# Second block of a two-block transformer: norm scales applied behind the products, norm rows multiplied beside the root

## The reference, cut to what matters

```python
def rmsnorm(x, g):
    return x * rsqrt(mean(x * x) + 1e-6) * g

for l in range(DEPTH):
    h = rmsnorm(x, g_pre_mix[l])
    y = mixers(h @ w_in[l])                      # three attention-like mixers
    x = x + rmsnorm(y @ w_out[l], g_post_mix[l])
    h = rmsnorm(x, g_pre_ffn[l])
    gate, up = split(h @ w_ffn_in[l])            # 2 x 2816 columns
    f = (silu(gate) * up) @ w_ffn_out[l]
    x = x + rmsnorm(f, g_post_ffn[l])
    e = p[l] @ w_ple_up[l]                       # 256 -> 1024
    g = sigmoid(rmsnorm(x, g_ple_gate[l]) @ w_ple_gate[l])
    x = x + rmsnorm(e * g, g_ple_post[l])
```

## Time and profile before

| | |
|---|---|
| median of three runs | 1909.09 us (1905.82 to 1911.23) |
| profiled execution | 1908.69 us, span 1906.9 us |
| PE busy | 1708.8 us, 90% of the span |
| DVE busy | 1093.6 us, 57% |
| ACT busy | 720.8 us, 38% |
| chain that ended last | PE 78%, DVE 13%, ACT 5%, issue 3% |
| second block | from about 1085 us to the end |

### The profile page before, as it was taken

One profiled execution on the slowest core, in us unless ns is written; L12 is line 12 of the kernel. 1 busy time (PEld: TensorE's weight loads), 2 busy tenths in 40 slices (PEclk: granted clock), 3 DMA queues, 4 the chain that ended last, 5 costly groups with the idle time before them and its releaser, 6 DMA issues.

```text
span 1906.9 us, 19158 instructions
## 1 busy us (share of the span) xinstructions
PE 1708.8 (90%) x7483; PEld 1287.3 (68%) x7483; DVE 1093.6 (57%) x1659; ACT 720.8 (38%) x1084; POOL 0.2 (0%) x4
## 2 busy tenths in 40 slices
PE   2999889999997998899999869889997798899995
PEld 2545647788884446477888757768885677788874
DVE  7574558686655625585455456754554457554544
ACT  1122333334321123343344235743444556543444
POOL 0000000000000000000000000000000000000000
PEclk9998689999998996899999979889998899899997
DMA  8655324876854441247555633134563352335540
GB/s 320 244 192 196 110 84 153 304 272 241 281 204 143 177 155 66 70 163 258 170 169 197 228 74 126 45 133 163 170 241 132 118 149 74 133 118 170 176 166 22
DMA packets 216378, 314.98 MB, mean 165 GB/s; under 512 B 20308, under 2 KB 145628, under 8 KB 216160
## 3 DMA queue, kind: packets, MB, share of 16 engines
q1 hardware_dynamic: 216288, 313.76, 47.8%
HBM read 312.70 MB, written 1.05 MB: 165 GB/s over the span
## 4 chain that ended last, share of the span: by engine, by line
PE 78%; DVE 13%; ACT 5%; issue 3%; SPq 0%; DVEq 0%; DMA 0%; ACTq 0%
PE psum L537 18%; PE psum L538 18%; PE psum L539 17%; PE psum L503 10%; DVE tmp L1150 3%; PE psum L544 2%; DVE arena L1150 1%; ACT arena L2071 1%; PE psum L580 1%; PE psum L1033 1%; PE psum L523 1%; PE psum L524 1%; PE psum L525 1%; DVE arena L1147 1%; ACT arena L2074 1%
## 5 line engine op out<-in xcount | busy, mean ns | idle before, releaser
L539 PE MATMUL psum<-arena_parts,hT_parts 128*128 128x512 f32 x928 | 370.1, 399 | 0.0
L1147 DVE TENSOR_TENSOR gring_parts<-gring,arena_parts 128x2048 fp32r<-128x2048 f32 x116 | 260.4, 2288 | 86.0 <-ACT arena_parts L2074 86.0
L503 PE MATMUL psum<-gring,hT 128*128 128x512 f32 (+1 forms) x576 | 256.7, 605 | 12.4 <-DVE arena L1147 6.1
L538 PE MATMUL psum<-gring_parts,arena_parts 128*128 128x512 f32 x544 | 221.7, 408 | 0.0
L1147 DVE TENSOR_TENSOR arena_parts<-psum,ex_parts 128x256 fp32r<-128x256 f32 x108 | 45.2, 418 | 299.6 <-ACT ex_parts L2074 299.6
L2074 ACT ACTIVATE arena_parts<-gring 128x2048 fp32r<-128x2048 f32 x116 | 215.4, 1917 | 0.1
L537 PE MATMUL psum<-arena_parts,o_cat_parts 128*128 128x512 f32 x512 | 205.9, 402 | 7.2 <-DVE hT_parts L1147 7.2
L503 PEld LDWEIGHTS psum<-gring,hT 128*128 128x128 f32 x576 | 114.1, 202 | 140.1 <-issue 122.0
L539 PEld LDWEIGHTS psum<-arena_parts,hT_parts 128*128 128x128 f32 x928 | 177.5, 191 | 41.9
L538 PE MATMUL psum<-gring_parts,o_cat_parts 128*128 128x512 f32 x512 | 204.9, 400 | 0.0
L2074 ACT ACTIVATE ex_parts<-psum 128x256 fp32r<-128x256 f32 x108 | 41.3, 382 | 416.3 <-PE psum L580 416.3
(11 more groups left out here) (218 smaller groups left out, 2296.7 us busy)
## 6 DMA issues: line engine op xcount, KB each, us to landing
gring<-in_w_ada SPq DMA_DIRECT2D x24, 2048.0 KB, 9.9
gring<-in_w_ffn_in SPq DMA_DIRECT2D x44, 1024.0 KB, 8.8
gring<-in_w_gate SPq DMA_DIRECT2D x32, 1024.0 KB, 7.4
gring<-in_w_up SPq DMA_DIRECT2D x32, 1024.0 KB, 9.8
dring<-in_w_down SPq DMA_DIRECT2D x32, 1024.0 KB, 5.0
gring<-in_w_in SPq DMA_DIRECT2D x14, 2048.0 KB, 10.5
dring<-in_w_ffn_out SPq DMA_DIRECT2D x22, 1024.0 KB, 4.9
gring<-in_w_out SPq DMA_DIRECT2D x8, 2048.0 KB, 8.5
```

The source lines that it names most:

```text
L503: last = nc.tensor.matmul(ps[:, 0:n], hT[:, k, t * P:(t + 1) * P], w[:, k, 0:n], start=k == 0, stop=k == KT - 1)
L538: nc.tensor.matmul(ps, hi, w_rest, start=False, stop=False)
L539: return nc.tensor.matmul(ps, lo, w, start=False, stop=stop)
L1147: return nc.vector.tensor_tensor(o, a, b, op)
```

## The change

- Pre-norm before the feed-forward part and before the embedding gate: x itself is transposed and multiplied by the gain column. The square sum of x, its root and its reciprocal are made behind that (`scale_squares`, `scale_of`, `scale_root`, `scale_done`), and the reciprocal is applied to the products: as the scale of the Silu and of the Sigmoid activation, and as a column factor in `hid`.
- Post-norm: each half is first multiplied by the row alone, the second half between the variance and the reciprocal, that is beside the root; then one instruction multiplies by the reciprocal and adds to x (`gained_and_added`, `rms_var`, `rms_added`).
- The transposes of tile 1 (xT2) go between the two halves of gu(0, 0); the transposes xT3 go behind the embedding products of their tile.
- pg0 takes the place of pg1 in steps 9 and 10; pg1 is rounded in step 10 (ScalarE) and its rest made around hT3 (VectorE). pg0 lies where pg1 did, pg1 in the other weight buffer.
- The embedding products are read from PSUM by VectorE instead of being copied by ScalarE; pg takes banks 4 to 7.
- avcv of the following layer is rounded before the Sigmoids; its rest is made before them too.
- Table loads are asked for early by one-element activations (`table_of`).
- SP: the small parameters of the following layer wait for the last product pg(1, 1); before, for the last gu.

```diff
-IN_DOWN = ("avcv", "aq", "ak", "buv", "cqk", "wo0", "pg0")
+IN_DOWN = ("avcv", "aq", "ak", "buv", "cqk", "wo0")
...
             if name == "pg1":
-                return stage, T, ("gu1", NF - 2)
-            if name == "pg0":
-                return stage, T, ("e", 1, 1)
+                return stage, T, ("gu1", NF - 1)
             if name == "avcv":
-                return (FIRST[-1], T, ("dn1", NE - 2 + q)) if stage == SECOND[0] else (SECOND[0], T, ("pg", 1, 0))
+                return (FIRST[-1], T, ("dn1", NE - 2 + q)) if stage == SECOND[0] else (SECOND[0], T, ("e", 1, 1))
...
-                        transposed("xT2", o_cat, 0, 6, ("xn", "ffn", 0))
+                        transposed("xT2", x, 0, 6, ("x", "mix", 0))
...
             first_half_gu(stage, 0, range(4, 8))
+            transposed("xT2", x, 1, 2, ("x", "mix", 1))
             first_half_gu(stage, 0, range(4)).then_inc(tensor_done, T.step(("gu0", 0)))
-            transposed("xT2", o_cat, 1, 2, ("xn", "ffn", 1))
...
-                    ps = take(("e", t, h), A, 2 * t + h)
+                    ps = take(("e", t, h), V, 2 * t + h)
...
-            transposed("xT3", o_cat, 0, 4, ("xn", "ple", 0))
+                transposed("xT3", x, t, 4 + 2 * t, ("x", "ffn", t))
...
-                        tt(hid[:, t, :], up, sact[:, t, :], ALU.mult)...
+                        stt(hid[:, t, :], up, scale[:, t:t + 1], sact[:, t, :], ALU.mult, ALU.mult)...
...
+        def rms_added(name, t, y):
+
+            dve.wait_ge(scalar_done, A.at(V, (("post", name), "sqrt", t)))
+            nc.vector.reciprocal(rstd[:, TT + t:TT + t + 1], rstd[:, t:t + 1])...
+            dve.wait_ge(vector_done, V.now())
+            stt(x[:, t, :], y, rstd[:, TT + t:TT + t + 1], x[:, t, :], ALU.mult, ALU.add)...
+
+        def gained_and_added(name, row, t, y, banks):
+
+            for h in range(2):
+                ps, read = banks(h)
+                if h:
+                    rms_var(("post", name), t)
+                else:
+                    dve.wait_ge(scalar_done, A.at(V, (("post", name), "ss0", t)))
+                tt(y[:, t, h * N:(h + 1) * N], ps, rows[:, row, h * N:(h + 1) * N], ALU.mult)...
+            rms_added(name, t, y[:, t, :])
...
+            for t in range(TT):
+                gained_and_added("mix", 0, t, y2m, lambda h: (bank(V, ("wo", t, h)), ("read", ("wo", t, h))))
+                modulated("xT2", "hT2", t, g_ffn)
+                features_rest("hT2", t, h_hi[1])
+                scale_of("ffn", t)
+                scale_done("ffn", t)
...
+            for t in range(TT):
                 modulated("xT3", "hT3", t, g_ple)
                 features_rest("hT3", t, h_hi3)
+                scale_of("ple", t)
+                chunk_rest(stage, "pg1", t)
+            for t in range(TT):
+                scale_done("ple", t)
+            following = SECOND[l + 1] if l + 1 < DEPTH else None
+            if following:
+                for q in range(2):
+                    chunk_rest(following, "avcv", q)
...
+            act.wait_ge(vector_done, V.at(A, ("scale", "ffn", TT - 1)))
+            act_experts(NF, 1, first_gate, scaled, second_gate)
...
+            for t in range(TT):
+                scale_root("ple", t)
+            following = SECOND[l + 1] if l + 1 < DEPTH else None
+            if following:
+                for q in range(2):
+                    rounded_half(following, "avcv", q)
+            table_of(ACT.Sigmoid)
...
             gated(0, 0)
+            squares(0, 0)
             gated(0, 1)
+            table_of(ACT.Sqrt)
+            squares(0, 1)
+            root_of(("post", "ple"), rstd[:, 0:1], 0)
...
-                sp.wait_ge(tensor_done, T.of(SECOND[l - 1], ("gu1", NF - 1)))
+                sp.wait_ge(tensor_done, T.of(SECOND[l - 1], ("pg", 1, 1)))
```

More of the change, by code:

```diff
@@ L451, in program @@
         rsum2, rinv2, ngm2 = sc(TT * 2 * DH), sc(TT * 2 * DH), sc(TT * WH)
+        scale_ss, scale_var, scale, idle = sc(TT), sc(TT), sc(TT), sc(1)
         lprod = sc(2 * DQK)
@@ L1714, in pre_norm, with scale_of, scale_done @@
             dve.wait_ge(vector_done, V.now())
-        def post_norm(name, row, t, y, banks):
-            rms(("post", name), t, True)
+        def scale_of(name, t):
+            dve.wait_ge(scalar_done, A.at(V, (("scale", name), "ss", t)))
+            ts(scale_var[:, t:t + 1], scale_ss[:, t:t + 1], 1.0 / D, RMS_EPS, ALU.mult, ALU.add).then_inc(vector_done, V.step((("scale", name), "var", t)))
+        def scale_done(name, t):
+            dve.wait_ge(scalar_done, A.at(V, (("scale", name), "sqrt", t)))
+            nc.vector.reciprocal(scale[:, t:t + 1], scale_var[:, t:t + 1]).then_inc(vector_done, V.step(("scale", name, t)))
+            dve.wait_ge(vector_done, V.now())
@@ L1982, in embedded @@
+                tt(y2[:, t, n], y2[:, t, n], bank(V, ("e", t, h)), ALU.mult).then_inc(vector_done, V.step(("eg", t, h)))
+                V.also(("read", ("e", t, h)))
                 dve.wait_ge(vector_done, V.now())
-                tt(x[:, t, :], x[:, t, :], y2[:, t, :], ALU.add).then_inc(vector_done, V.step(("x", "ple", t)))
-                dve.wait_ge(vector_done, V.now())
-            following = SECOND[l + 1] if l + 1 < DEPTH else None
+                tt(gb[:, n], y2[:, t, n], rows[:, 0, n], ALU.mult).then_inc(vector_done, V.step())
@@ L2440, in act_second @@
             for t in range(TT):
-                for h in range(2):
-                    act.wait_ge(tensor_done, T.at(A, ("e", t, h)))
-                    ps = bank(A, ("e", t, h))
-                    copy((e2 if t == 0 else e2b)[:, h * N:(h + 1) * N], ps).then_inc(scalar_done, A.step(("read", ("e", t, h))))
-            for q in range(2):
-                rounded_half(stage, "pg0", q)
-            for t in range(TT):
-                act.wait_ge(vector_done, V.at(A, ("x", "ffn", t)))
-                sum_squares(("pre", "ple"), t, x)
-                modulated_T("xT3", "hT3", t, g_ple, hi=h_hi3)
+                act.wait_ge(vector_done, V.at(A, ("x", "ffn", t)))
@@ L2452, in gated @@
+                scale_squares("ple", t)
+                modulated_T("xT3", "hT3", t, g_ple, hi=h_hi3)
+            for t in range(TT):
+                scale_root("ple", t)
[4 more added lines that the diff above has]
+            table_of(ACT.Sigmoid)
             def gated(t, h):
                 act.wait_ge(tensor_done, T.at(A, ("pg", t, h)))
-                activate(y2[:, t, h * N:(h + 1) * N], bank(A, ("pg", t, h)), ACT.Sigmoid).then_inc(scalar_done, A.step(("sig", t, h)))
+                if h == 0:
+                    act.wait_ge(vector_done, V.at(A, ("scale", "ple", t)))
+                    act.sem_inc(waited)
+                activate(y2[:, t, h * N:(h + 1) * N], bank(A, ("pg", t, h)), ACT.Sigmoid, **scaled(t)).then_inc(scalar_done, A.step(("sig", t, h)))
```

111 lines of the change are left out of this document (56 added, 55 removed).

## The result

The changed kernel took 1862.74 us (median of four runs, 1858.2 to 1866.43); the kernel before, on the same chip, 1908.82 us (1905.82 to 1911.23). The ratio is 0.9758, 95% interval 0.9733 to 0.9784: 46 us less, where 40.5 were forecast. The profiled execution took 1862.91 us, its span 1861.1. TensorE's busy time fell from 1708.8 to 1697.8 us for the same number of instructions, so most of what went is idle time, the rest slow clock.

A forecast was written before the change was run, and what follows sets the result against it. TensorE was taken to be bound by waits at each layer's two joints and the second layer's entry, plus slow clock behind idle times. Gains 3.4 + 1.7 + 18.7 + 16.7 = 40.5 us gave 1868.5 us, range 1859 to 1879.

The forecast's parts named there:

- rival (a): Joint A: the clock holds through the 3.9 us idle time, 2 x 2.4 us more gained, 1863.7; 12 in 100.
- Joint B: Last down product to pg's end: waits before transposes and pg go; 14.7 us gained in layer 1, 14.8 in layer 2.
- End: Second layer's last product to the last x: 5.4 us instead of 7.3, saving 1.9.
- Steps: Expert steps: column factor in hid and column scale in Silu, 22 times each, lie under TensorE's work; cost 0.
- The slow stretch behind gu(1,0)'s idle time: Step 1's first products, each layer: the clock falls after some 3.9 us idle, costing 12 x 0.2 = 2.4 us.
- Joint A: Out projection to step 1: gu(1,0) starts 5.8 us earlier in layer 1, 4.1 in layer 2; net 3.4 and 1.7.
- Entry: Pg's end to the second layer's first avcv products: 18.7 us gained, including joint B's 14.7.
- (b): Joint B: pg is held up by supplies 3 us late, plus a 2.4 us slow stretch per layer; 1879; 10 in 100.
- (d): Joint B's and gu(0)'s products run at the lower clock throughout, slower than before at 1926; 2 in 100.
- (c): Entry gains nothing beyond pg's 14.7, as avcv's roundings and a table load precede the first Sigmoid; 1872.5; 13 in 100.
- (e): Whole kernel: the new code doesn't do what it says, x being waited for anyway; no change, 1909; 1 in 100.
- The drain of 1.38 us on every table switch: Rule weighed, not adopted: with three table loads before avcv(0), the entry would be some 4 us later, the sum 36.

The follow-up runs named there:

- e2: Changed kernel with pre-norm's scale applied in front again at joint B only (scaled copy transposed, Sigmoid without scale); 1873.52 us, ratio 0.982.
- e3: Changed kernel with row and reciprocal in one product behind the root, then the addition, at every post-norm, as before; 1870.82 us, ratio 0.9804.
- e5: Changed kernel with both halves of pg1 rounded behind the last step's squares instead of in the steps; 1863.18 us, ratio 0.9779.
- e9: Changed kernel with the edits of e1, e2, e3 and e5 together, avcv left early; 1884.72 us, ratio 0.9882.
- e8: Changed kernel with ScalarE copying the four embedding banks to SBUF again and VectorE reading them there; 1865.11 us, ratio 0.9778.
- e1: Changed kernel with pre-norm's scale applied in front again at joint A only (scaled copy transposed, Silu and hid without scale); 1867.99 us, ratio 0.9796.
- e4: Changed kernel with step 1's weights split early, before Silu (0,0); 1850.38 us, ratio 0.9704.
- e6: Changed kernel with the following layer's avcv rounded and its rest made behind Sigmoid (1,0) instead of ahead of the Sigmoids; 1863.98 us, ratio 0.9776.
- e7: e4 plus, at the entry to the second layer, tile 0's hT and its rest made ahead of Sigmoid (1,1) and its product; 1848.12 us, ratio 0.9691.

## Why the prediction was right, and which of its terms were off

Forecast 1868.5 (1859 to 1879), measured 1862.74. The mechanism held at both joints, the entry and the end; the sum was 5 us short. That is a net figure: stretch by stretch, about 9 us went beyond the forecast and 3.6 were lost that it hadn't. That the two partly cancel is luck, and the measured time lies nearer to rival (a)'s 1863.7 than to the forecast.

**Right.** Joint B: 14.7 and 14.8 forecast, 14.9 and 15.0 measured. The supplies of pg came in time, PEclk was 1.00 over all of it, pg took 22.33 and 22.30 us. e2, e3, e5 and e9 divide it: 6.0 to 6.4 from the scale behind the products, 0.5 from the row product, 1.9 to 2.2 from pg1's place, 1.4 and 0.8 from their overlap, 2.4 from the order that e9 keeps, and 2.5 and 2.7 from pg at the full clock; e8's part is nothing at this joint. End: 1.9 forecast, 2.15 measured, of which e3 gives back 1.25; the last product starts at 1852.68 and x's last instruction at 1856.78, as these rows of PE and DVE in after show, to be set beside the earlier trace rows:

```profile
1852.68 0.39 PE L539 MATMUL psum<-arena_parts,hT_parts 128*128 128x512 f32 x1
...
1856.78 1.28 DVE L1148 SCALAR_TENSOR_TENSOR x<-gb,small,x 128x1024 f32<-128x1024 f32 x1
```

Steps: 0 forecast, 0.15 lost a layer, all of it in the last step, where the down products of tile 1 wait 0.15 us for the rest of hid; e1 and e9, whose hid has no column factor, don't lose it (171.58 and 171.57). The Silu with a column scale takes 0.48 us instead of 0.38, in chains that TensorE doesn't wait for. The parameters' first use had no wait: SP issues them from here on in after, and the first use is at 1505.31, 24 us later.

```profile
1480.95 0.82 SPq L2557 DMA_DIRECT2D arena<-in_lam_q  x2
```

**The slow stretch behind gu(1,0)'s idle time: forecast 2.4 twice, measured 1.6 and 0.** This is the largest error, 3.2 us in the direction of rival (a), which had 12 in 100 and came half true. I had taken it from the clock falling behind each idle time over 2.2 us of the block before. The idle time itself was forecast at 3.9 and was 3.3.

**Joint A: forecast 5.8 and 4.1, measured 6.5 and 5.2.** The chain was the one described. From the square of wo(0,1) to the table load that precedes Silu the forecast has 1661.3 - 1640.45 = 20.85 us, and the timeline above 1636.55 - 1616.57 = 19.98. The pieces: x 3.05 behind the square's start, not 3.4, in both tiles; idle before the transposes of tile 1 0.46, not 0.8; from the end of the square of x (1635.77) to the load 0.78, where its read and the small instructions were put at 1.14. From the load to gu(1,0) it is 8.16, where 1669.4 - 1661.3 = 8.1 was forecast. e1 adds what the forecast didn't divide: of this gain 4.2 us hang on the scale, e3 says 2.7 on the row product, and e4 shows that another 6.8 were to be had in the same place for a change of order. The forecast's words "the bound then changes" need care: the way from table load over Silu to step 1's weights ended 0.57 us ahead of gu(1,0) in the kernel before too (1672.92 and 1673.49), and it binds e1's second layer. The change uncovered it more than it made it.

**Entry: forecast 4.0 beyond joint B, measured 5.4** (5.7 to avcv(0), 1.0 to avcv(1), less 1.3 behind it). The forecast has avcv(0) 6.4 us behind the end of the last pg product; it came 5.0 behind. Sigmoid (1,1) ran right behind pg's end, 0.2 us for 2.2 in the forecast, since tile 0 was ahead: avcv's rest was done 1.5 us and x 2.0 us sooner before pg's end than put down. From there to avcv(0) it took 4.8 us, not 4.2. e6 shows 3.25 of the 5.7 to come from the roundings' place.

**Mixers of the second layer: forecast 0, lost 1.9.** Nothing there was changed. In the kernel before the same stretch has

```profile
1530.80:1609.50 78.70, 69.45 (x518) 59.55 (x516) 51.30 (x85) 51.61 (x108) 0.00 (x0) 1.00 0.44 134
```

against 80.30 us, PE busy 71.10 and PEclk 0.97 in after. Over all kernels the whole mixers took from 97.75 to 101.26 us, and e2, e3, e4 and e7 show 97.8. The 1.60 us between these two stretches are covered by TensorE's extra 1.65 us of busy time at the lower granted clock, so it is the clock; why one kernel loses more there than another these runs don't show.

**Rivals.** (b) and (d) are excluded by pg's stretch, (c) by e6, (e) by the result. The drain of 1.38 us on every table switch, which the Trainium skill states (ScalarE: Activation LUTs, "What ACT_TABLE_LOAD costs"), is not seen in any timeline here: in after the load starts at 1636.55, lasts 1.28, and the activation behind it starts at 1637.85. By it the entry would have been an estimated 4 us later; it was 1.4 earlier than the sum without it.

## What to carry to other kernels

When a scale is taken out of the chain ahead of products, it comes back in the consumer's chain: ask at once what the consumer's engine has to do behind it before the following product. Here that chain (load, Silu, next weights) was close to binding already, and taking the weights out of it was worth 6.8 us and a slow stretch (e4). Two edits that shorten one chain must be sized with the other in place: the scale at joint A was worth 4.2 us, not the 8 to 10 that the waits of before suggest. And read an edit of a few microseconds stretch by stretch between the same products, since untouched stretches of this kernel differ by as much from kernel to kernel.

## What the runs showed of the hardware

**The same idle time doesn't give the same clock.** Before gu(1,0), TensorE was idle some 3.3 us in both layers of after, e2, e3, e5, e6 and e8: twelve cases with the same 24 products behind. In three the clock stayed up (5.65 to 5.67 us), in six it fell for some products (7.23), in three for more (8.15 to 8.24). So behind 3.3 us the price was 0, 1.6 or 2.6 us, on average (6 x 1.6 + 3 x 2.6) / 12 = 1.45. The idle 2.54 and 3.12 us in e2's first layer left the transposes behind them at 1.06 us, while 2.52 us in its second layer slowed them to 1.58, and 1.88 us in the kernel before to 1.61: the length of one gap doesn't decide it.

**The clock moves stretches far from any edit.** In the first 300 us, the same code in both, the granted clock was 0.88 in after and 0.93 in e1 (first after, then e1; columns as above):

```profile
0.00:300.00 300.00, 238.63 (x830) 144.15 (x831) 181.87 (x405) 67.67 (x126) 0.20 (x4) 0.88 0.54 193
```

```profile
0.00:300.00 300.00, 239.71 (x862) 146.48 (x863) 188.33 (x412) 69.81 (x129) 0.20 (x4) 0.93 0.55 195
```

e1 had started 32 products more by then, and reached the first wo product at 1226.64 us, after at 1231.34. That is 4.7 us of a span, near the 5.7 that this kernel's measurement can't tell from no change.
